# Gathering the tokens of two experts with one product of 256 one-hot columns, with the loops over pairs of experts written out

## What is computed

```
logits = xf @ w_router;  top_v, top_i = top_k(logits, 2);  w = softmax(top_v)
gate = sum(one_hot(top_i, 8) * w[..., None], axis=1)
for e in range(8):
    out = out + gate[:, e:e+1] * swiglu(xf, w_in[e], w_out[e])
```

## Time and profile before

| | us |
|---|---|
| median of 3 runs | 2717.24 |
| lowest, highest | 2713.71, 2718.2 |
| the profiled execution's own time | 2718.97 |
| its span from the first to the last instruction | 2717.2 |
| TensorE busy in the span | 2608.8 |
| VectorE busy | 2104.6 |
| ScalarE busy | 1580.1 |

### The profile page before, as it was taken

The page is one execution under the profiler, slowest core; times in us unless marked ns, Lnnn a source line. Parts: engine busy times, 40 slices in busy tenths (PEclk is TensorE's granted clock), DMA queues, the critical chain, the costliest instruction groups (busy, mean ns, idle before and its releaser), DMA issues.

```text
span 2717.2 us, 40101 instructions
## 1 busy us (share of the span) xinstructions
PE 2608.8 (96%) x13300; PEld 2128.4 (78%) x13300; DVE 2104.6 (77%) x2469; ACT 1580.1 (58%) x2048; POOL 21.5 (1%) x39
## 2 busy tenths in 40 slices
PE   7999899999999999999998988999999999999997
PEld 5777788887777897788997766878788878888875
DVE  6777777787767666676557766898899989999998
ACT  3555444456544454354444554777777777777775
POOL 0000000000000000000000000000000000000000
PEclk9999999999999999999998897999999999999998
DMA  8665568666644665454563405999999989999995
GB/s 310 226 211 178 189 208 283 225 211 198 201 160 165 226 217 182 147 202 150 186 216 132 127 32 207 330 357 341 329 342 339 360 310 363 328 364 330 367 354 205
DMA packets 190553, 666.17 MB, mean 245 GB/s; under 512 B 22880, under 2 KB 30688, under 8 KB 189776
## 3 DMA queue, kind: packets, MB, share of 16 engines
q1 hardware_dynamic: 186512, 647.66, 68.3%
q0 software_dynamic: 3904, 16.76, 1.9%
HBM read 663.29 MB, written 1.05 MB: 244 GB/s over the span
## 4 chain that ended last, share of the span: by engine, by line
PE 83%; DVE 8%; DVEq 3%; ACT 2%; DMA 2%; issue 2%; SPq 0%; ACTq 0%
PE ps L511 40%; PE ps L517 20%; PE ps L936 7%; PE ps L943 3%; PE ps L536 3%; DVE wlo L2158 2%; PE ps L618 1%; PE ps L544 1%; PE ps L1374 1%; ACT whi L1508 1%; DVE mod_sum L2182 1%; DMA ada_raw<-in_w_ada 1%; DVEq L2656 1%; DMA proj<-in_w_ada 1%; DVE xl L2241 1%
## 5 line engine op out<-in xcount | busy, mean ns | idle before, releaser
L2158 DVE TENSOR_TENSOR wlo<-raw,whi 128x1024 fp32r<-128x1024 f32 x674 | 820.3, 1224 | 382.2 <-ACT whi L1508 373.8
L1508 ACT ACTIVATE whi<-raw 128x1024 fp32r<-128x1024 f32 x674 | 710.6, 1060 | 625.7 <-PE ps L517 458.1
L511 PE MATMUL ps<-whi,gathered_hi 128*128 128x512 f32 x896 | 362.3, 404 | 2.6 <-DVE att L2441 1.8
L511 PE MATMUL ps<-whi,gathered_lo 128*128 128x512 f32 x896 | 355.6, 397 | 0.0
L517 PE MATMUL ps<-wlo,gathered_hi 128*128 128x512 f32 x896 | 283.2, 397 | 3.9 <-DVE wlo L2158 3.9
L511 PE MATMUL ps<-whi,xh 128*128 128x512 f32 (+2 forms) x704 | 282.5, 402 | 3.4 <-ACT proj L1548 3.4
L511 PE MATMUL ps<-whi,xl 128*128 128x512 f32 (+2 forms) x704 | 274.0, 390 | 0.0
L511 PE MATMUL ps<-whi,yh 128*128 128x512 f32 (+2 forms) x592 | 237.3, 403 | 6.5 <-DVEq L2277 3.2
L511 PE MATMUL ps<-whi,yl 128*128 128x512 f32 (+2 forms) x592 | 228.0, 388 | 0.0
L2158 DVE TENSOR_TENSOR wlo<-spare,whi 128x1024 fp32r<-128x1024 f32 x168 | 204.6, 1225 | 19.0 <-ACT whi L1508 17.4
L2158 DVE TENSOR_TENSOR wlo<-mod_b,whi 128x1024 fp32r<-128x1024 f32 x168 | 205.4, 1223 | 16.8 <-ACT whi L1508 11.8
(11 more groups left out here) (437 smaller groups left out, 4234.3 us busy)
## 6 DMA issues: line engine op xcount, KB each, us to landing
raw<-in_moe_w_in SPq DMA_DIRECT2D x227, 512.0 KB, 5.0
spare<-in_moe_w_in SPq DMA_DIRECT2D x165, 512.0 KB, 5.4
mod_b<-in_moe_w_out SPq DMA_DIRECT2D x165, 512.0 KB, 5.3
raw<-in_w_ff SPq DMA_DIRECT2D x120, 512.0 KB, 4.4
raw<-in_w_in SPq DMA_DIRECT2D x96, 512.0 KB, 4.2
work<-in_moe_w_in SPq DMA_DIRECT2D x56, 512.0 KB, 5.3
work<-in_moe_w_out SPq DMA_DIRECT2D x56, 512.0 KB, 4.8
ada_raw<-in_w_ada SPq DMA_DIRECT2D x48, 512.0 KB, 4.4
```

Source lines behind the costliest of these rows:

```text
L511: e.matmul(ps[0:lhs[2], banks[t], at:at + width], part[:, k0 + j, t * P:t * P + lhs[2]], whi[:, slot, w], start=first and j == 0 and part ...
L1508: e.activation(whi[:, slot, :], src, ACT.Copy).then_inc(split_hi, 1)
L2158: e.tensor_tensor(wlo[:, slot, :], src, whi[:, slot, :].bitcast(F32), ALU.subtract).then_inc(split_lo, 1)
```

## The change

One one-hot matrix of 256 columns now holds the places of two experts, and a job of the gather has four products of 256 columns in place of eight of 128. The gathered inputs of a pair lie in one buffer of 256 places, and the second such buffer is `xh`/`xl`, which are not used otherwise at that time. The eight jobs of a pair (`pair_columns`) run in the second and third step of the second expert of the pair before; each expert's own two turns of `onehot` (`own_rows`) stay in the second step. The first pair is gathered whole ahead of the first step. Because a pair's index selects the buffer, the eight experts are written out on all engines, with constant indices; the three copies of `place`, `sel` and `gate` into `now` are gone. The inner loop has three steps in place of four where the third step is written out.

```
-        gathered = [[sb(f"gathered_{part}{b}", [P, KB, P], F32R) for part in ("hi", "lo")] for b in range(2)]
+        gathered = [[sb(f"gathered_{part}", [P, KB, 2 * P], F32R) for part in ("hi", "lo")], [xh, xl]]
-        onehot = [sb(f"onehot{b}", [P, NT, P], F32R) for b in range(2)]
+        onehot = sb("onehot", [P, NT, 2 * P], F32R)
...
+                def gathered_of(i):
+                    pair = gathered[i // 2 % 2]
+                    return tuple(part[:, :, i % 2 * P:(i % 2 + 1) * P] for part in pair) + (P,)
+                def pair_columns():
+                    def columns(q, part):
                         def fill(e, bank):
-                            for j in range(4):
-                                k = half * 4 + j
+                            for j in range(2):
+                                k = q * 2 + j
                                 for t in range(NT):
-                                    mm = e.matmul(ps[:, bank, j * P:(j + 1) * P], part[:, t, k * P:(k + 1) * P],
-                                                  onehot[b][:, t, :], start=t == 0, stop=t == 1)
+                                    mm = e.matmul(ps[:, bank, j * 2 * P:(j + 1) * 2 * P], part[:, t, k * P:(k + 1) * P],
+                                                  onehot[:, t, :], start=t == 0, stop=t == 1)
...
+                    elif b == 0:
+                        clear(e)
+                        step(e, now_, hid, EXPERT, {5: [turned] + own_rows(1), 7: [clear]})
                     else:
-                        job_of = gather(1 - b)
+                        pair = pair_columns()
                         clear(e)
-                        step(e, now_, hid, EXPERT, {0: [source, job_of[0], job_of[1]], 1: job_of[2:3],
-                                                    2: job_of[3:4], 3: [clear], 5: [turned] + job_of[4:6], 7: [clear]})
+                        step(e, now_, hid, EXPERT, {0: [source, pair[0], pair[1]], 1: pair[2:3], 2: pair[3:4], 3: [clear],
+                                                    5: [turned] + own_rows(0), 7: [clear]})
+                        step(e, now_, hid, EXPERT, {0: pair[4:6], 1: pair[6:7], 2: pair[7:8], 3: [clear]})
+                        steps -= 1
+                    if not last:
                         e.sem_inc(pe_tick, 1)
-                    loop(e, c, D_FFE // 512 - 3, lambda e, s: step(e, now_, hid, EXPERT))
+                    loop(e, c, steps, lambda e, s: step(e, now_, hid, EXPERT))
...
-                    for piece in gather(0):
+                    for piece in pair_columns() + own_rows(0):
...
-                    loop(e, c, N_EXP // 2 - 1, two)
-                    one_expert(e, 0)
-                    one_expert(e, 1, last=True)
+                    for i in range(N_EXP):
+                        one_expert(e, i, last=i == N_EXP - 1)
...
-                def tokens_of(e, i, b):
-                    at = bass.ds(i, 1)
-                    e.tensor_copy(now[b][:, 0:2].rearrange("p (t o) -> p t o", o=1), place[:, :, at])
-                    e.tensor_copy(now[b][:, 2:4].rearrange("p (t o) -> p t o", o=1), sel[:, :, at])
-                    e.tensor_copy(now[b][:, 4:6].rearrange("p (t o) -> p t o", o=1), gate[:, :, at])
-                    e.drain()
-                    for t in range(NT):
-                        e.tensor_scalar(onehot[b][:, t, :], k_("iota"), now[b][:, t:t + 1], now[b][:, 2 + t:3 + t],
-                                        ALU.is_equal, ALU.mult)
+                def tokens_of(e, i):
+                    for b in range(2):
+                        for t in range(NT):
+                            e.tensor_scalar(onehot[:, t, b * P:(b + 1) * P], k_("iota"), place[:, t, i + b:i + b + 1],
+                                            sel[:, t, i + b:i + b + 1], ALU.is_equal, ALU.mult)
                     to_pe(e)
...
-                    pieces[8].append(lambda e: e.drain())
-                    if not last:
-                        pieces[9] = [lambda e: tokens_of(e, i + 1, 1 - b)]
+                    if i % 2 and not last:
+                        pieces[9] = [lambda e: tokens_of(e, i + 1)]
```

More of the change, by code:

```diff
@@ L2043, in output, with one_expert @@
                         e.activation(eh[:, n * 512:(n + 1) * 512], ps[:, 2 + n, :], ACT.Copy).then_inc(out_hi, 1)
-                def one_expert(e, b, last=False):
+                def one_expert(e, i, last=False):
+                    second, third = ({}, {}) if last else gather_pieces(jobs, plain, i)
                     output(e)
                     step(e, hidden_e[0], EXPERT)
-                    step(e, hidden_e[0], EXPERT, {} if last else gather_pieces(jobs, gather_jobs(plain, 1 - b)))
-                    loop(e, c, D_FFE // 512 - 3, lambda e, s: step(e, hidden_e[0], EXPERT))
+                    step(e, hidden_e[0], EXPERT, second)
+                    if third:
+                        step(e, hidden_e[0], EXPERT, third)
+                    loop(e, c, D_FFE // 512 - (4 if third else 3), lambda e, s: step(e, hidden_e[0], EXPERT))
                     if not last:
@@ L2057, in one_round @@
                     e.activation(st[:, 30:31], k_("eps"), ACT.Silu)
[L2058 removed]
+                    jobs(e, pair_copies(plain, 0) + row_copies(plain, 0))
                     pass_units(e, 8)
@@ L2094, in act_program, with pair_copies, row_copies, gather_pieces @@
                 act.activation(st[:, 8 + t:9 + t], st[:, t:t + 1], ACT.Sqrt).then_inc(last_root, 1)
[L2097 to L2108, removed]
-            for t in range(NT):
-                out_.append(plain(onehotT[b][:, t * P:(t + 1) * P], lambda bank: ps[:, bank, 0:P]))
-            return out_
+        def pair_copies(plain, i):
+            return [plain(gathered[i // 2 % 2][part][:, 2 * q:2 * q + 2, :],
+                          lambda bank: ps[:, bank, :].rearrange("p (k s) -> p k s", k=2))
+                    for q in range(KB // 2) for part in range(2)]
+        def row_copies(plain, b):
+            return [plain(onehotT[b][:, t * P:(t + 1) * P], lambda bank: ps[:, bank, 0:P]) for t in range(NT)]
+        def gather_pieces(jobs, plain, i):
+            def of(copy):
+                return [lambda e: jobs(e, [copy])]
+            second = {6 + t: of(copy) for t, copy in enumerate(row_copies(plain, (i + 1) % 2))}
+            if i % 2 == 0:
+                return second, {}
+            pair = pair_copies(plain, i + 1)
+            second.update({n: of(pair[n]) for n in range(4)})
+            return second, {n: of(pair[4 + n]) for n in range(4)}
         def own_head_turns(plain):
@@ L3254, in add_output, with one_expert @@
                     return [part(t, n) for n in range(2) for t in range(NT)]
[L3256 removed]
+                def one_expert(e, i, last=False):
                     output(e)
[L3258 to L3261 removed]
+                    pieces = {5 + n: [piece] for n, piece in enumerate(add_output(i - 1))}
+                    if i % 2 and not last:
+                        pieces[9] = [lambda e: tokens_of(e, i + 1)]
+                    second, third = ({}, {}) if last else gather_pieces(jobs, plain, i)
                     step(e, hidden_e, EXPERT, pieces)
[L3263 to L3264 removed]
+                    step(e, hidden_e, EXPERT, second)
+                    if third:
+                        step(e, hidden_e, EXPERT, third)
+                    loop(e, c, D_FFE // 512 - (4 if third else 3), lambda e, s: step(e, hidden_e, EXPERT))
                     if not last:
@@ L3271, in one_round @@
                 def one_round(e, r):
-                    tokens_of(e, 0, 0)
-                    e.tensor_scalar(now[1], now[0], 0.0, None, ALU.mult)
+                    tokens_of(e, 0)
+                    e.tensor_scalar(no_gate, gate[:, 0, 0:2], 0.0, None, ALU.mult)
                     e.tensor_scalar(onehotT[1][:, :], x[:, 0, 0:S], 0.0, None, ALU.mult)
-                    jobs(e, gather_jobs(plain, 0))
+                    jobs(e, pair_copies(plain, 0) + row_copies(plain, 0))
                     pass_units(e, 8)
@@ L3278, in one_round @@
                     make_hidden(e, EXPERT)
-                    def two(e, i):
-                        one_expert(e, i * 2, 0)
-                        one_expert(e, i * 2 + 1, 1)
-                    loop(e, c, N_EXP // 2 - 1, two)
-                    one_expert(e, N_EXP - 2, 0)
-                    one_expert(e, N_EXP - 1, 1, last=True)
+                    for i in range(N_EXP):
+                        one_expert(e, i, last=i == N_EXP - 1)
                     output(e)
-                    for piece in add_output(1):
+                    for piece in add_output(N_EXP - 1):
                         piece(e)
```

31 lines of the change are left out of this document (15 added, 16 removed).

## The result

The changed kernel took 2692.43 us (median of four, 2690.91 to 2700.46) beside 2716.39 for the kernel before: ratio 0.9911, 95% interval 0.9895 to 0.9928, that is 24 us or 0.89% faster where 18.7 us were foretold. Over all 20 times of the changed kernel the median is 2697.4 us and the mean 2696.6; the four medians of the kernel before lie between 2715.8 and 2717.1. So the lasting gain is 18.5 us by the medians of all times and 19.7 us by the means.

A forecast was written before the change was run, and what follows sets the result against it. TensorE's stream of products was taken to bound the kernel. From 2717.2 us, -7.6 (A), -2.6 (B), -9.3 (C) and +0.8 (D) gave 2698.5 us; range 2694.5 to 2704, or to 2706.5 with rival 1, another cause of VectorE's idle time.

The forecast's parts named there:

- Part A: Outer loops over expert pairs written out: removes two returns of VectorE's loop at 3.8 us each, -7.6 us.
- Rival 4: Expert stage: TensorE's straight code arrives late at 12 places, 3.8 us each; 2744.1 us; chance 0.05.
- Rival 5: Steps: another engine's time per step takes the freed time, no lasting gain; about 2716 us; chance 0.03.
- TensorE's own return: At the outer loop's return TensorE showed no idle time of its own; no term hangs on a fetch there.
- Part C: Gathers of the other three pairs: number of products counts, not width; -3.1 us a pair, -9.3 us.
- Part D: Steps with jobs: shorter jobs give bank copies less cover, small waits at six places; +0.8 us in all.
- rival 3: At six places TensorE waits 0.5 us or more for a copy and the clock falls; 2711.7 us; chance 0.06.
- Part B: First pair's gather: second expert's jobs leave the first expert's second step; -2.6 us, bounds -3.5 and -1.0.
- the head: Gather ahead of the steps: 32 products of 256 columns at half clock, 6.8 us as before, plus 0.8 for copies.
- The sum: Whole kernel: -18.7 us from the profile's 2717.2, taken as the median, gives 2698.5 us; chance 0.77.

The follow-up runs named there:

- TensorE's long body: Kernel before with VectorE's outer loop written out and TensorE's inner loops written out inside its kept outer loop: 2716.13 us, ratio 0.9996.

## Why the prediction came out as it did

**Part A** was right in place and size: 3.8 us a return, no new idle time in the straight code. Rival 4, late straight code, did not occur in any kernel with both outer loops written out. Rival 5, another engine taking the freed time, is out as well: the seven windows are 19.5 us shorter. The weak point of the argument, TensorE's own return, was open; the run with TensorE's long body closes it.

**Part C** was right: foretold 9.3 for three pairs. Each pair's two windows went from 254.6 us without a return to 251.6, 251.8 and 252.2, together 8.2 us with part D in it, foretold 8.5.

**Part D** was right in place and small. The waits before the turn of the hidden tile (line 618) are there, in the changed kernel's waits from 1815 to 2565 us (total, times, longest):

```profile
PEld ps L618 <- issue: 3.2, 6, 0.6
```

Six of them, as foretold. The profile names no releaser for them. With 128 columns throughout, where a job covers its copy for longer, the same waits are nearly gone (from 1828 to 2591 us):

```profile
PEld ps L618 <- issue: 0.3, 2, 0.2
```

The products behind the six start 0.19 to 0.36 us late, 1.6 us in all, where 0.6 was counted and 3.0 was the bound. The clock stayed at 1.00 in all windows, so rival 3 is out. Spread over four steps the jobs no longer cause them: window 4 is 127.38 us, 0.7 less.

**Part B** failed in one term, the head. The step was "It runs at half clock ... 6.8 us in all, as before", with +0.9 for copies and one-hot parts. Two things in it were wrong, in opposite directions. The price at half clock was taken from the router's products with 8 stationary columns, 0.212 us; with 128 stationary columns it is 0.25 us, a job of four 1.0 us and not 0.85, and eight jobs at that clock would be 8.0 us and not 6.8. What makes the difference between the two rows is not shown. And half clock is no property of the place: it held through 32 or 64 products of 128 columns in every one of eight profiles, and ended 3.2 to 6.2 us after the first product of 256 columns in six of six. The second outweighed the first. From the first product to `clear_sums` it was 2.5 or 0.2 us less than before, not 0.9 more. The term was mis-sized by 1.1 to 3.4 us, and its bounds did not take in a clock that rises.

**The sum** failed in the step from the profile to the median, "the rows may stand for the median as they are". Its range took 4.5 us of scatter in all, from three runs, so some 2.2 to each side. The 20 times of the changed kernel spread over 11.6 us, and its four medians lie between 2692.4 and 2698.9. The experts start anywhere in ten microseconds, roughly as the granted clock of the stretch before goes, while no instruction differs. The first result had three of four times between 2690.9 and 2693.4 us; the 16 later ones fill the stretch from 2691.2 to 2702.5. The mean of 20, 2696.6 us, lies in the range and 1.9 us from the forecast. That the first result lay outside was in part the head (on the mean of four profiles 1.4 us less than before, 2.3 less than foretold) and in part chance. How large a share of that first median each of them had is not to be told from four times.

## What to carry to other kernels

Look at what one product costs at either width before merging products: where 128 columns cost 0.105 us and 256 cost 0.119, halving the count is worth nearly half the time. Take that price from rows of the same form: at half clock 256 columns cost 0.212 us with 8 stationary columns and 0.25 with 128. Cut the trace into windows at the same place of each turn of a loop: two windows out of seven that were 3.8 us longer gave the returns away, and the fix could be tried on one engine at a time. For a gain under 1% compare stage by stage from the first changed instruction on, and with several profiles, since the rest of the program moves by more than the term in question.

## What the runs showed of the hardware

In the gather ahead of the experts the granted clock stayed at 0.50 through 64 products of 128 columns without a gap (13.7 us, two profiles), and for some 4 us of products of 512 columns behind them. With 256 columns in the same place it rose 3.2 to 6.2 us after the first product, in six profiles of six; in one of them only 16 such products stood there and the rise came 2.3 us into the first unit. The six profiles with 32 products of 128 columns stayed at 0.50 too, but their gather took only 6.8 us, so the two with 64 carry the point. Width and number of products changed together, and which of them counts is not shown.

A return of the outer loop cost VectorE 3.5 to 4.5 us of idle time, whether its inner loops were loops or written out. It cost TensorE 2.55 and 2.71 us once its inner loops were written out inside the body, and nothing that shows before. The releaser named for TensorE's idle time was wrong, as the engine named had long been done.
